# Mixing phase of a hybrid decoder layer: probabilities turned in blocks of 32 on VectorE, value products on four row groups of TensorE

## The reference, cut to what matters

```python
s = jnp.einsum('btngd,btknd->btngk', q, k_sel) * (B_HD ** -0.5)
s = jnp.where(valid[:, :, None, None, :], s, -jnp.inf)
p = jax.nn.softmax(s, axis=-1)
return jnp.einsum('btngk,btknd->btngd', p, v_sel)
```

## Time and profile before

| | before |
|---|---|
| median of 3 executions | 4006.8 us (4002.0 to 4010.09) |
| the profiled execution | span 4000.7 us from its first to its last instruction; its own time is not given apart from the three |
| TensorE busy over the span | 3854.3 us (96%) |
| VectorE, ScalarE busy over the span | 2916.5 us, 1411.3 us |
| mixing phase | 834 us, TensorE busy in 785 of them |

### The profile page before, as it was taken

One profiled execution on the slowest core, in us unless ns is written; L12 is line 12 of the kernel. 1 busy time (PEld: TensorE's weight loads), 2 busy tenths in 40 slices (PEclk: granted clock), 3 DMA queues, 4 the chain that ended last, 5 costly groups with the idle time before them and its releaser, 6 DMA issues. The chain is left out here.

```text
span 4000.7 us, 41769 instructions
## 1 busy us (share of the span) xinstructions
PE 3854.3 (96%) x14518; PEld 2310.1 (58%) x14518; DVE 2916.5 (73%) x3866; ACT 1411.3 (35%) x2593; POOL 1672.7 (42%) x1529
## 2 busy tenths in 40 slices
PE   7899999999999999999999799999997999999999
PEld 4555555564456566665665566555553788854444
DVE  5589999689999999999996566555454577653333
ACT  5411211155334423433431666555553322111121
POOL 0000045459687656665654332122103766552111
PEclk9999999999999999999999899999997999999999
DMA  6312222420111121211211633232232855531111
GB/s 221 92 60 65 67 87 86 142 95 37 61 61 68 50 71 64 71 63 66 72 58 59 194 120 99 70 88 77 61 102 87 226 168 171 169 128 69 40 53 46
DMA packets 290039, 368.31 MB, mean 92 GB/s; under 512 B 72635, under 2 KB 217619, under 8 KB 286630
## 3 DMA queue, kind: packets, MB, share of 16 engines
q1 hardware_dynamic: 249434, 249.73, 20.7%
q0 software_dynamic: 19664, 86.31, 5.9%
q10 hardware_dynamic: 20736, 29.66, 2.3%
HBM read 235.04 MB, written 129.28 MB: 91 GB/s over the span
## 5 line engine op out<-in xcount | busy, mean ns | idle before, releaser
L1315 DVE MAX8 best<-score 128x8 f32<-128x384 f32 (+13 forms) x448 | 639.7, 1428 | 23.3 <-POOL score L1283 8.3
L1317 DVE MATCH_REPLACE8 score<-best,score 128x384 f32<-128x384 f32 (+13 forms) x448 | 631.2, 1409 | 0.0
L1072 PE MATMUL pr<-xnT,w_row 128*128 128x347 f32 (+1 forms) x960 | 298.3, 457 | 0.0
L1224 POOL TENSOR_TENSOR kT<-kT 128x347 f32<-128x347 f32 (+1 forms) x240 | 193.8, 808 | 215.2 <-ACT kT L1142 208.4
L396 PE MATMUL pg<-xnT,wt 128*128 128x416 f32 x800 | 281.8, 515 | 0.0
L1700 PE MATMUL mix_slot<-mix_kT,mix_bq 128*128 128x512 f32 (+3 forms) x640 | 271.6, 540 | 7.7 <-DVE mix_sd L2039 3.2
L1739 PE MATMUL mix_po<-mix_probT,mix_v 128*128 128x512 f32 x544 | 240.4, 595 | 5.2 <-ACT mix_probT L1839 4.3
L1072 PEld LDWEIGHTS pr<-xnT,w_row 128*128 128x128 f32 x960 | 180.3, 190 | 106.6 <-issue 10.0
L1142 ACT COPY kT<-pr 128x347 f32<-128x347 f32 (+1 forms) x240 | 106.7, 446 | 352.9 <-PE pr L1072 342.5
L396 PEld LDWEIGHTS pg<-xnT,wt 128*128 128x128 f32 x800 | 152.6, 191 | 127.6 <-issue 127.6
L1224 POOL TENSOR_TENSOR kT<-kT,sm 128x347 f32<-128x347 f32 (+1 forms) x179 | 159.7, 892 | 124.7 <-ACT sm L1142 121.7
(11 more groups left out here) (636 smaller groups left out, 8048.0 us busy)
## 6 DMA issues: line engine op xcount, KB each, us to landing
gt_scr<-kT SPq DMA_DIRECT2D x40, 694.0 KB, 3.3
out_gm<-gt_scr ACTq DMA_DIRECT2D x32, 520.0 KB, 5.3
gt_scr<-kT SPq DMA_DIRECT2D x20, 692.0 KB, 4.2
wt<-in_w_in SPq DMA_DIRECT2D x22, 512.0 KB, 4.0
...
```

The costliest lines, as they stand in the source:

```text
L1072: ins = nc.tensor.matmul(pr[:, b, 0:w], lhs, rhs, start=k == 0, stop=k == 3)
L1224: nc.gpsimd.tensor_tensor(o[:, slot, :], o[:, slot, :], term, ALU.add).then_inc(added, 1)
L1315: nc.vector.max(best[:, :], sc).then_inc(top_step, 1)
L1317: nc.vector.match_replace(sc, best[:, :], sc, TAKEN).then_inc(top_step, 1)
```

## The change

Attention now runs in 32 units of four heads and one query block: all 16 blocks for key head 0, then all 16 for key head 1. Their probabilities lie in a ring of 16384 columns, which the largest two units nearly fill. For each unit:

- S: pieces of 512 columns, each in one bank; there are three slots, which the memory steps share. M2, M3 and M4 go head by head (one matmul and one slot each), and the turned keys of M1 take a slot of their own (MT).
- E(n) stands right behind the pieces of S(n); N(n-1) follows, and the last head of a unit has N(n) at once. N on VectorE is the reciprocal alone; ScalarE multiplies the row (a copy with a scale).
- X: VectorE turns each 32 x 32 block of a head's probabilities in place.
- H and O are the two halves of a unit's value products. Values are loaded four times, once for each 32 partitions, so row group a (partitions 32a to 32a + 31) holds 32 keys per block, and its matmul makes the results of 32 queries of each of four heads (128 columns) in its own bank of `po`. 16 matmuls of 32 rows and 128 columns take the place of one of 128 rows and 512 columns. Two heads' scores of the next unit stand between H and O, except where the ring is full: there H and O follow each other.
- Keys and values of one key head are resident; those of head 1 are loaded in the middle of the phase. Queries and mask are loaded per unit.

The transposes on TensorE, their evacuations, `probT` and the two `pg` banks go.

```diff
+GQ = BH // KV
+MIX_UNITS = [(kv, i) for kv in range(KV) for i in range(NB)]
+MIX_HEADS = GQ * len(MIX_UNITS)
+BLK = 32
+QUADS = P // BLK
+RING_COLS = 8 * SEQ
+RECENT = 8
+SLOTS = 3
...
+def ring_places():
+    at, after, cursor = [], [], 0
+    for u, (_, i) in enumerate(MIX_UNITS):
+        size = GQ * (i + 1) * P
+        if cursor + size > RING_COLS:
+            cursor = 0
+        shared = [w for w in range(u) if at[w] < cursor + size and cursor < at[w] + GQ * (MIX_UNITS[w][1] + 1) * P]
+        at.append(cursor)
+        after.append(max(shared, default=-1))
+        cursor += size
+    return at, after
...
+    sample, memory = sample_events(), memory_steps()
+    assert max(sample) < MIX_HEADS and max(memory) < MIX_HEADS
+    _, after = ring_places()
+    events, waiting, turned = [], [], 0
+    def begin_products(u):
+        nonlocal turned
+        while turned <= min(u + 1, scored):
+            events.extend(("X", GQ * turned + h) for h in range(GQ))
+            turned += 1
+        events.append(("H", u))
+    def end_products(u):
+        events.append(("O", u))
+    scored = -1
+    for u, (kv, i) in enumerate(MIX_UNITS):
+        ahead = 2 if u == 0 or 0 < i < 6 else 1
+        begun = None
+        while waiting and (waiting[0] <= after[u] or len(waiting) > ahead):
+            begun = waiting.pop(0)
+            begin_products(begun)
+            if (waiting and (waiting[0] <= after[u] or len(waiting) > ahead)) or begun <= after[u]:
+                end_products(begun)
+                begun = None
+        for h in range(GQ):
+            n = GQ * u + h
+            if h == 2 and begun is not None:
+                end_products(begun)
+            events.append(("S", n, 0))
+            events += memory.get(n, [])
+            if n in sample:
+                events.append(sample[n])
+            events += [("S", n, q) for q in range(1, key_pieces(n))]
+            events.append(("E", n))
+            if h:
+                events.append(("N", n - 1))
+        events.append(("N", n))
+        waiting.append(u)
+        scored = u
+    for u in waiting:
+        begin_products(u)
+        end_products(u)
...
-        slot = ps("slot", [P, 2, 1024])
-        pg, po, pb = ps("pg", [P, 2, 512]), ps("po", [P, 512]), ps("pb", [P, 512])
-        k_resident, v_resident = ([sem(f"{n}_resident{x}") for x in range(2)] for n in "kv")
+        slot = ps("slot", [P, SLOTS, 512])
+        po, pb = ps("po", [P, QUADS, 512]), ps("pb", [P, 512])
...
+            def load_keys(kv, lo, hi):
+                at = slice(lo * P, hi * P)
+                sp.dma_start(kT[:, at], d["qt"][T_BK + kv, :, at]).then_inc(k_resident[2 * kv + (lo > 0)], 16)
+            def load_values(kv, lo, hi):
+                col = R_BKV + KV * HD + kv * HD
+                src = d["r"][lo * P:hi * P, col:col + HD].rearrange("(n k) e -> k n e", k=BLK)
+                for a in range(QUADS):
+                    sp.dma_start(v[BLK * a:BLK * a + BLK, QUADS * lo:QUADS * hi, :], src).then_inc(v_resident[2 * kv + (lo > 0)], 16)
...
+                if e[0] == "S" and e == last_piece(e[1] // GQ):
+                    u = e[1] // GQ
+                    if u + 2 < UNITS_OF_MIX:
+                        load_a(u + 2)
+                    if u == NB - 1:
+                        after_slot(sp, e)
+                        load_keys(1, 0, FIRST_KEYS)
+                        load_keys(1, FIRST_KEYS, NB)
+                elif e[0] == "M4" and e[2] == AH - 1 and e[1] + 2 < NB:
+                    load_m(e[1] + 2)
+                elif e == ("O", NB - 1):
+                    sp.wait_ge(values_used, 1)
+                    load_values(1, 0, FIRST_KEYS)
+                    sp.wait_ge(o_mm, NB)
+                    load_values(1, FIRST_KEYS, NB)
...
+            def values_times_probs(u, half):
+                kv, i = MIX_UNITS[u]
+                at, blocks = unit_probs(u), QUADS * (i + 1)
+                if half == 0:
+                    pe.wait_ge(v_resident[2 * kv + (i >= FIRST_KEYS)], 16 * QUADS)
+                    pe.wait_ge(turned, GQ * (u + 1))
+                    if u:
+                        pe.wait_ge(oT_ready, u)
+                for b in range(half * (blocks // 2), blocks if half else blocks // 2):
+                    for a in range(QUADS):
+                        rows = slice(BLK * a, BLK * a + BLK)
+                        ins = mm(po[:, a, 0:GQ * BLK], v[rows, b, :], at[rows, :, BLK * b:BLK * b + BLK], start=b == 0, stop=b == blocks - 1)
+                    if u == NB - 1 and b == QUADS * FIRST_KEYS - 1:
+                        ins.then_inc(values_used, 1)
+                if half:
+                    ins.then_inc(o_mm, 1)
...
-                    for t in range(i + 1):
-                        ins = mm(po[:, :], v[:, t, kv * HD:(kv + 1) * HD], probT[:, t, :, :], start=t == 0, stop=t == i)
-                    ins.then_inc(o_mm, 1)
...
-            nc.scalar.copy(probT[:, t0:t1, hd % 4, :],
-                 pg[:, n % 2, 0:(t1 - t0) * P].rearrange("p (t q) -> p t q", q=P)).then_inc(bank_free[n % 2], 1)
...
+                elif kind == "N":
+                    act.wait_ge(inverse, i + 1)
+                    nc.scalar.activation(probs(i), probs(i), ACT.Copy, scale=rsum[:, i % RECENT:i % RECENT + 1]).then_inc(normed, 1)
...
-                    nc.vector.tensor_scalar(prob[b][:, 0:(i + 1) * P], prob[b][:, 0:(i + 1) * P], rsum[:, e[2]:e[2] + 1], None,
-                                            ALU.mult).then_inc(normed, 1)
...
+                elif kind == "X":
+                    dve.wait_ge(normed, i + 1)
+                    nc.vector.transpose(probs(i), probs(i)).then_inc(turned, 1)
```

407 lines of the change are left out of this document (170 added, 237 removed).

## The result

The changed kernel takes 4086.6 us in the median of four runs (4083.4 to 4090.4), the kernel before 4004.4 us beside it (4001.8 to 4010.1): ratio 1.0205, 95% interval 1.019 to 1.0219. It is slower by 82 us, where 35 us were forecast. The profiled execution spans 4084.5 us.

What follows compares the result with a forecast made beforehand. TensorE was taken to set the mixing phase's pace; -118.6 (transposes) - 20.5 (idle) + 8.0 (products) + 16.4 (form changes) + 150 (new waits) = +35.3, so 4000.7 + 35.3 + 6.1 = 4042 us, range 3930 to 4120.

Steps and rivals of the forecast that it cites:

- Transposes, products, changes of form: TensorE work in the mixing phase: transposes removed -118.6 us, value products +8.0, switching the array's row form +16.4.
- The bound of two groups: Value products: if only two row groups overlap, they take twice 241.5 us; four were assumed.
- The turn at VectorE: VectorE's 32 x 32 turn of probabilities: 2.2 us at 2048 columns, about 165 us in all.
- VectorE's sum 527: VectorE's busy time in the mixing phase: 440 - 114 + 165 + 36 = 527 us, not the bound by its sum.
- ScalarE unchanged: ScalarE's total hardly moves: it gives up 153.7 us of evacuations and gains about 140 us of normalising copies.
- is it hidden where it stands?: Asks whether VectorE and ScalarE work stays covered by TensorE at each place; new waits were put at 150 us.
- Double units, 72 us: Four places with two units without products between: +18 us of TensorE waits each, 72 us.
- Single units, units 9 to 11, small heads, the output buffer: Other new waits: 12 single units 36 us, units 9 to 11 12, small heads 12, the only output buffer 8.
- Loads and half clock, 10 us: Value loads ahead of the queries of units 2 and 18, and half clock behind the four long waits: 10 us.
- TensorE does not stay the bound: Rival that TensorE stays the bound, nearly all waits covered: 3932 us, chance 0.32; decided at 115 us of new waits.
- Row groups overlap: Rival that row groups do not fully overlap in the value products: 4122 us for the milder case, chance 0.09.
- the turn is not twice as dear: Rival that VectorE's turn costs twice a column cycle, +145 us of VectorE: 4136 us, chance 0.07.

Runs made afterwards that it cites:

- run 5: Changed kernel with the value products run over two row groups at a time instead of four: 4470.3 us, ratio 1.1171 to the kernel before.
- run 4: Changed kernel without VectorE's 32 x 32 turn, products using probabilities that are not turned: 4043.5 us, ratio 1.0096 to the kernel before.
- run 10: Changed kernel with the normalising pass moved back from ScalarE to VectorE: 4112.1 us, ratio 1.0263 to the kernel before.
- run 15: Changed kernel with turns spread over the next unit's heads only where two units stand in a row: 4072.1 us, ratio 1.0173 to the kernel before.
- run 6: Changed kernel with each unit's products left whole, both halves standing where the first stood: 4092.9 us, ratio 1.0225 to the kernel before.
- run 8: Changed kernel with value loads spread out, pairs' first-unit products moved into the second unit, each unit's last normalising behind the next unit's first head: 4076.8 us.
- run 9: Changed kernel with 60 of the 64 pairs of gathers of cached pages left out of the phase: 4081.7 us, ratio 1.0194 to the kernel before.
- run 11: Changed kernel with the store of y issued three heads later: 4091.4 us, ratio 1.0207 to the kernel before.
- run 13: Changed kernel with y stores and memory-tile loads issued later, and queries and mask too from the unit of six blocks on: 4081.0 us, ratio 1.0179.
- run 3: Changed kernel with extra unread TensorE matmuls during the waits before the products of units 12, 14, 28 and 30: 4096.0 us, ratio 1.0229.

## Why the forecast was right in sign and short in size

*Transposes, products, changes of form: -118.6 + 8.0 + 16.4 = -94.2.* Measured -93.9 at full clock. The bound of two groups is excluded by run 5. A full-clock run of 448 records takes 12.79 us, 0.114 for four, where 0.111 was taken: 7 us more. The change of form is 0.29 us and not 0.4: 4 us less. Some 3 us of slow feeding had no term, and in other programs it is up to 13. That is 6 us more, so 6 us of other work went that no row names: the size of this term is right, and the agreement to 0.3 us is luck.

The Trainium skill, "TensorE: Matmul & The Clock Gate", section "Part 3: Packing small matmuls", gives 3.07 times for four groups at 512 columns; by it, an estimate, the products would have taken 73 us more. No run here has that width. At 128 columns this case's trace does not agree: per row of keys the four groups run at the pace of the full array (four records of 32 rows in 0.114 us, one record of 128 rows and 128 columns in 0.111), so the measurement decides.

*The turn at VectorE, 2.2 us and 165 in all:* 2.27 and 155. *VectorE's sum 527:* 514. *ScalarE unchanged:* 478 against 475. The three rates that had no row of their own (the turn, ScalarE's normalising at 149 us against 140, four row groups) came out within 7%. No idle time went in run 4 beyond the pairs, so "is it hidden where it stands?" had the right answer: in single units yes, in pairs no.

*Double units, 72 us:* these eight units stand idle for 81.1 us, in which is what the kernel before had there: it stood idle for 26 of the 736 us from 2300 us on, 3.6%, which makes 12 us. (The text has 2%, and most of its 49 idle us at the start; more than half lie behind 2300.) So 69 against 72: right, with gaps of 10.6 to 12.7 us where 10 were named. The reason given, VectorE's 36 us of work for eight heads, is half wrong: it is not full in the second unit (run 10). What stands bare is the order: the last exponential and the first four of eight turns in one place, the 7.6 us that the text has for the turns (7.4 in the trace; runs 4 and 15).

*Single units, units 9 to 11, small heads, the output buffer: 36 + 12 + 12 + 8 = 68.* All idle time rose by 134.7; less the pairs' 69, the mask's 35.3 and the holes' 17.4 this leaves 13, to which come the 20.5 that went with the transposes: about 33 us against 68. Too much by 35, and by luck this hides two fifths of the miss that follows.

*Loads and half clock, 10 us:* **the step that failed.** It came to 35.3 us of waits for the mask, 39.3 us of half clock and 17.4 us of holes in the feeding, 92 us against 10. The cause of the first stood in the text, 8 MB of values in a queue ahead of the queries of units 2 and 18; nobody worked out what 3 MB ahead of a small load cost. (The second wait hit unit 20, whose loads stood behind the second 3 MB.) For the second, the text looked at the four long waits only. They hold a small part: the four stretches at half clock beside them have 3.0, 3.3, 3.1 and 5.1 us of TensorE's work, and the other 19 have 84 of the 98 us. 14 of these stand behind waits of 2.0 to 4.2 us and have 60 us, and the sum had priced each such wait at its own length. The third was not thought of.

So 35.3 - 3 - 35 + 82 gives 79, and the phase grew by 80. *The rivals:* TensorE does not stay the bound. Its decision point was 115 us of new waits; the new waits are the 134.7 and the 20.5 that went, 155 us, and the clock's 39 come on top. Row groups overlap and the turn is not twice as dear. The other phases kept their times to 4 us and not to one or two: 968 us after the phase against 964, in windows whose edges I set by hand, with the 4 us in the first 104.

## What stays open

What holds up a fetch of instructions for 7 us. The hole in unit 23's products came at the same record in the changed kernel and in runs 6, 8, 9, 10, 11 and 13 and in no other; in the changed kernel it starts at 2837.6 us, with the DMA engines little busy until 2841 (their share in fortieths of 2834 to 2846 us, then the queues):

```profile
DMA  9995511146300111000122322267899999999999
...
q1 hardware_dynamic: 1840, 1.20, 35.5%
q0 software_dynamic: 305, 0.97, 20.4%
q8 instruction: 1, 0.02, 0.5%
```

A test would be the same products in a program with half the instructions; none was tried. That the holes end with a fetch is seen 43 times; no run changes fetches alone. What makes slow feeding is open altogether. It comes at the same places or hardly at all, in programs that differ elsewhere, and in run 3's unit 5 (2341.7 to 2347.4) no fetch falls: the last starts at 2332.8 and the next at 2348.8. It accounts for most of the 8 us by which programs differ in a stretch that neither changes (run 3).
